# One order for the mixers' steps and the weight stream, set by an expected time per engine

## The reference

```
for l in range(2):                                   # second block
    p = rms_norm_2(h, norm_pre_mix[l]) @ w_in[l]     # 2048 x 7952
    o_ret  = retention_group(p_ret)
    o_hgrn = hgrn2_group(p_hgrn, ...)
    o_ml   = mlstm_group(p_ml, ...)
    o_rw, v_first = rwkv7_group(p_rw, v_first, ...)  # delta rule: a triangular solve in chunks of 128
    h = h + rms_norm_2(concat([o_ret, o_hgrn, o_ml, o_rw]) @ w_out[l], norm_post_mix[l])
    u = rms_norm_2(h, norm_pre_ffn[l])
    h = h + rms_norm_2((silu(u @ w_gate[l]) * (u @ w_up[l])) @ w_down[l], norm_post_ffn[l])
```

## Time and profile before

| | |
|---|---|
| device time, 3 runs | median 4277.95 us (4275.65 to 4281.48) |
| the profiled execution's own time | 4288.42 us |
| its span, first to last instruction | 4287.1 us |
| mean granted TensorE clock | 0.951 of full speed |
| HBM read | 623.04 MB, 146 GB/s over the span |

### The profile page before, as it was taken

The page is one execution under the profiler, slowest core; times in us unless marked ns, Lnnn a source line. Parts: engine busy times, 40 slices in busy tenths (PEclk is TensorE's granted clock), DMA queues, the critical chain, the costliest instruction groups (busy, mean ns, idle before and its releaser), DMA issues.

```text
span 4287.1 us, 57523 instructions
## 1 busy us (share of the span) xinstructions
PE 3928.6 (92%) x24004; PEld 3484.0 (81%) x24004; DVE 2291.8 (53%) x3630; ACT 1784.1 (42%) x2539; POOL 106.7 (2%) x61
## 2 busy tenths in 40 slices
PE   6999988998899899778999999989898779999998
PEld 5777766877688888558999988878787569999987
DVE  4455655566555554556555544565644665454444
ACT  4444534444443443324444444444433334444443
POOL 0000000000010000000000000010000000000000
PEclk9999999999999999869999999999999689999999
DMA  5555444554354433314666666544333136666665
GB/s 183 172 153 164 127 128 122 145 162 138 114 158 128 135 112 106 99 59 143 182 183 184 183 200 194 170 123 144 105 108 94 53 108 182 183 182 186 193 194 168
DMA packets 342084, 628.88 MB, mean 147 GB/s; under 512 B 21712, under 2 KB 64672, under 8 KB 340800
## 3 DMA queue, kind: packets, MB, share of 16 engines
q1 hardware_dynamic: 330888, 609.46, 47.8%
q10 hardware_dynamic: 10936, 15.75, 1.2%
HBM read 623.04 MB, written 2.10 MB: 146 GB/s over the span
## 4 chain that ended last, share of the span: by engine, by line
PE 78%; DVE 11%; ACT 6%; issue 2%; POOL 2%; ACTq 1%; DMA 0%; DVEq 0%; POOLq 0%
PE bank L453 66%; DVE weights_low L377 3%; ACT weights_high L375 2%; DVE arena L914 1%; PE bank L1076 1%; PE bank L1171 1%; PE bank L2191 1%; PE bank L2178 1%; PE bank L575 1%; PE bank L2190 1%; POOL stat L536 1%; DVE arena L1819 1%; PE bank L1079 1%; POOL arena L1786 1%; PE bank L1155 1%
## 5 line engine op out<-in xcount | busy, mean ns | idle before, releaser
L377 DVE TENSOR_TENSOR weights_low<-weights,weights_high 128x1024 fp32r<-128x1024 f32 (+4 forms) x1176 | 1399.2, 1193 | 1432.0 <-ACT weights_high L375 1425.3
L375 ACT ACTIVATE weights_high<-weights 128x1024 fp32r<-128x1024 f32 (+4 forms) x1176 | 1207.6, 1029 | 1275.7 <-PE bank L453 1246.6
L453 PE MATMUL bank<-x_high,weights_high 128*128 128x256 f32 x3776 | 1082.7, 287 | 28.2 <-DVE weights_low L377 12.3
L453 PE MATMUL bank<-x_low,weights_high 128*128 128x256 f32 x3776 | 1076.3, 285 | 0.0
L453 PE MATMUL bank<-x_high,weights_low 128*128 128x256 f32 x3776 | 1075.8, 285 | 0.0
L453 PEld LDWEIGHTS bank<-x_high,weights_high 128*128 128x128 f32 x3776 | 732.7, 194 | 38.1 <-DVE weights_low L377 25.0
L453 PEld LDWEIGHTS bank<-x_low,weights_high 128*128 128x128 f32 x3776 | 732.9, 194 | 0.0
L453 PEld LDWEIGHTS bank<-x_high,weights_low 128*128 128x128 f32 x3776 | 732.7, 194 | 0.0
L453 PE MATMUL bank<-weights_high,x_high 128*128 128x512 f32 (+3 forms) x1408 | 572.1, 406 | 69.2 <-DVE x_low L580 34.1
L453 PE MATMUL bank<-weights_high,x_low 128*128 128x512 f32 (+3 forms) x1408 | 547.1, 389 | 0.0
L453 PE MATMUL bank<-weights_low,x_high 128*128 128x512 f32 (+3 forms) x1408 | 546.7, 388 | 0.0
(11 more groups left out here) (377 smaller groups left out, 3677.4 us busy)
## 6 DMA issues: line engine op xcount, KB each, us to landing
weights<-in_w_in_dram SPq DMA_DIRECT2D x208, 512.0 KB, 3.7
weights<-in_w_ffn_gate_dram SPq DMA_DIRECT2D x176, 512.0 KB, 4.3
weights<-in_w_ffn_up_dram SPq DMA_DIRECT2D x176, 512.0 KB, 4.2
weights<-in_w_ffn_down_dram SPq DMA_DIRECT2D x176, 512.0 KB, 4.8
weights<-in_w_out_dram SPq DMA_DIRECT2D x128, 512.0 KB, 3.8
weights<-in_even_w_in_dram SPq DMA_DIRECT2D x88, 512.0 KB, 3.6
weights<-in_odd_w_in_dram SPq DMA_DIRECT2D x80, 512.0 KB, 3.7
weights<-in_mem_w_kv_dram SPq DMA_DIRECT2D x32, 512.0 KB, 4.4
```

Of the source, the lines that this page charges most:

```text
L375: dve.wait_ge(self.high_split.count(nc.scalar.activation(high, raw, ACT.Copy)))
L377: nc.vector.tensor_tensor(low, raw, high.bitcast(F32), ALU.subtract))
L453: ins = nc.tensor.matmul(out, l, r, start=(u == 0 and c == 0 and x + y == 0), stop=(u == blk.n - 1 and c == UNIT - 1 and y == 1))
```

## The change

**Expected time.** Each engine's queue (`Line`) gets a clock. Emitting an instruction adds a cost by its kind and its columns; counting up a semaphore records the clock plus 0.1 us as the expected time of that mark; a wait moves the waiting queue's clock up to it. `Matmuls` does this for PE.

**Pieces.** `step` now emits one bank of a unit instead of all of it: 6 matmuls of 512 or of 256 columns. The split of unit g+2 goes with a unit's first bank, the load of unit g+4 with its last; each bank of a block's last unit is evacuated as it is done.

**Order.** A task says before each of PE's waits which marks it will wait for (`yield wanted`); `rest` is gone, and a bare `yield` stands in its place. `weave` lets the stream go first only where `stream_first` says so: the task's marks are expected more than 0.7 us after the next piece could begin, or DVE's clock is over 3 us or ACT's over 2 us ahead of it. A bare `yield` so takes no piece of the stream unless DVE or ACT is ahead. `need` yields a constant that forces a piece each time. `fill` puts off a transpose whose mixer is expected to end more than 0.7 us after PE's clock, unless nothing else can go on. No computation changes, and no matmul, copy or transfer is added or removed.

```diff
+SLACK = 0.7
+DVE_LEAD, ACT_LEAD = 3.0, 2.0
+HOP = 0.1
+def expected_at(marks):
+    return max([expected.get((id(sem), value), 0.0) for sem, value in marks], default=0.0)
 class Line(Counter):
-    def __init__(self, eng, sem):
+    def __init__(self, eng, sem, start=0.16, column=0.00104):
     def wait_ge(self, *marks):
+        self.clock = max(self.clock, expected_at(marks))
+    def ran(self, ins):
+        n = columns(one.ins[0] if isinstance(one, mybir.InstTensorReduce) else one.outs[0])
+        self.clock += self.start + self.column * n * (6 if isinstance(one, mybir.InstReciprocal) else 1)
+class Matmuls(Line):
+    def matmul(self, out, lhsT, rhs, **flags):
+        self.clock += (n + 32) / 2400 if rhs.dtype == F32R else max(4 * n, 480) / 2400
+            self.act = Line(nc.scalar, sem("act_done"), 0.2, 0.00085)
+            self.pool = Line(nc.gpsimd, sem("pool_done"), 0.3, 0.0026)
-    def rest(self, us):
-        self.debt += us
-        while self.debt >= 1.3:
-            self.debt -= 1.3
-            yield
     def weave(self, task):
-        for _ in task:
-            self.fill()
-            stuck = 0 if self.step() else stuck + 1
+        for wanted in task:
+            if wanted == self.STREAM:
+                self.fill(True)
+                stuck = 0 if self.step() else stuck + 1
+                continue
+            self.fill(False)
+            while self.stream_first(wanted or []):
+                self.step()
+                self.fill(False)
+    def stream_first(self, wanted):
+        if self.g == len(self.units) or not self.can_run(*self.units[self.g]):
+            return False
+        marks = [self.load_mark[self.g] if blk.kind == "plain" else self.low_mark[self.g]]
+        begin = max(self.pe.clock, expected_at(marks))
+        return (expected_at(wanted) > begin + SLACK or self.dve.clock > begin + DVE_LEAD or self.act.clock > begin + ACT_LEAD)
     def fill(self, must):
-            if piece is not None and piece[0] in self.ended and self.blocks[piece[1]].done:
+            if piece is not None and piece[0] in self.ended and self.complete(piece[1]):
+                if not (must and i == 0) and expected_at(self.ended[piece[0]]) > self.pe.clock + SLACK:
+                    return
     def step(self):
-        self.g += 1
-        self.split(g + AHEAD)
-        marks = self.plain_unit(g, blk, u) if blk.kind == "plain" else self.matmul_unit(g, blk, u)
-        self.load(g + AHEAD + 2)
+        if n == 0:
+            self.split(g + AHEAD)
+        mark = self.plain_unit(g, blk, u) if blk.kind == "plain" else self.bank_matmuls(g, blk, u, n)
+        self.n += 1
+        if self.n == len(blk.banks):
+            self.g, self.n = g + 1, 0
+            self.load(g + AHEAD + 2)
         if u == blk.n - 1:
-            blk.done = [blk.evac(n, b, mark) for n, (b, mark) in enumerate(zip(blk.banks, marks))]
+            blk.done.append(blk.evac(n, blk.banks[n], mark))
...
+            yield [*self.bank_free[b]]
             pe.wait_ge(*self.bank_free[b])
-        yield from self.rest(3.0)
+        yield
...
-            if not (0 <= w < n and units[w].get("quiet")):
-                yield
```

More of the change, by code:

```diff
@@ L205 @@
     need: str = None
+    scale: object = None
     done: list = field(default_factory=list)
 class Program:
+    STREAM = "a piece of the stream"
     def __init__(self, nc, A, consts, out):
@@ L438, in matmul_unit, with bank_matmuls @@
+        return self.used_mark[g]
+    def bank_matmuls(self, g, blk, u, n):
+        pe, w, b = self.pe, blk.width, blk.banks[n]
         high, low = self.w_high[g % SPLIT], self.w_low[g % SPLIT]
[L439 to L456, removed]
@@ L1386, in indexer @@
             dve.wait_ge(dve.now())
-            yield from self.rest(1.4)
+            yield
         for t in range(T):
@@ L1634, in head_rms_gate @@
                 marks[t] = dve.did(nc.vector.tensor_tensor(tmp[:, t, :], tmp[:, t, :], gain, ALU.mult))
-            yield from self.rest(1.2)
+            yield
         for t in range(T):
@@ L1822, in hgrn @@
         exponents(0)
-        multiply(-1, k, q)
+        yield from multiply(-1, k, q)
         yield
@@ L1931, in mlstm @@
         yield
+        yield [m]
         pe.wait_ge(m)
@@ L2015, in rwkv @@
                 dve.seq(nc.vector.tensor_tensor(vc, vc, vf, ALU.add))
-                yield from self.rest(1.0)
+                yield
         else:
@@ L2080, in rwkv @@
             self.bank_free[b] = [m]
-        yield from self.rest(2.2)
+        yield
         L4 = L_.rearrange("p (n s) -> p n s", s=P)
@@ L2154, in rwkv @@
                     self.bank_free[b] = [m]
-                    yield from self.rest(0.9)
+                    yield
             for grp in range(2):
@@ L2270, in rwkv @@
         dve.seq(nc.vector.tensor_tensor(y3, y3, wide_st, ALU.subtract))
-        yield from self.rest(2.4)
+        yield
         act.wait_ge(dve.now())
@@ L2277, in rwkv @@
         dve.seq(nc.vector.tensor_tensor(y3, y3, wide_st, ALU.mult))
-        yield from self.rest(3.6)
+        yield
         dve.wait_ge(landed)
```

391 lines of the change are left out of this document (251 added, 140 removed).

## The result

| | before | after |
|---|---|---|
| median, 4 runs each | 4279.57 us (4275.65 to 4281.48) | 4109.95 us (4098.08 to 4116.59) |
| profiled execution | 4288.42 us | 4116.59 us |
| span | 4287.1 us | 4115.3 us |
| mean TensorE clock | 0.951 | 0.969 |

The ratio is 0.9602, 95% interval 0.9578 to 0.9625: 4.0 in 100 faster, 169.6 us by the medians, 171.8 by the profiled executions. The forecast was 4120.

What follows compares the result with a forecast made beforehand. PE was taken as the bound, busy 3928.6 of 4287.1 us. 151 + 32 + 43 - 70 = 156 us off the profiled 4288.4 gave 4132, or 4122 at the median, stated as 4120; range 4000 to 4262.

Steps and rivals of the forecast that it cites:

- part 3: hgrn and the first half of rwkv: finer pieces shorten what a mixer step waits behind; 32 of 94.6 us won.
- part 1: RWKV solves: stream only where PE would wait, so it fills the drains behind; 151 of 201.7 us won.
- rival 1: RWKV solve: the clock falls once the stream is thinned out there, slower than before, 4297 us; chance 0.10.
- rival 2: DVE becomes the bound: PE's waits for the stream's splits grow to some 75 us, +100, 4220; chance 0.16.
- rival 3: Everything is filled: drains give 180, the other two parts half of 238, slack costs 40; 259 off, 4020; chance 0.16.
- Part 2: Transposes behind mixers, mostly in the drains: putting them off removes 69 us of waits, already counted in the 151.
- part 4: The two attention layers with the memory: 43 us won of 143 idle and clock loss.
- Part 5: Some 850 places where PE can wait: SLACK leaves waits up to 0.7 us open, costing 70 us.
- rival 4: Mixers run ahead, then wait in `need` for inputs; the drains come back as long, no change; chance 0.04.

Runs made afterwards that it cites:

- The shift by itself: The kernel before, with only the two yields of each level of the RWKV solve taken out: 4217.6 us, ratio 0.9853.
- slack 0: The changed kernel with SLACK 0 for 0.7, so a piece goes in wherever PE would wait at all by the clocks: 4111.0 us, 0.9598.
- states fed: The changed kernel with one stream piece forced after each of the three steps of the chunk states behind the solve's levels: 4071.4 us, 0.9512.
- scaled thresholds: The changed kernel with expected costs of DVE, ACT and POOL halved, and SLACK and both leads halved too (0.35, 1.5, 1.0): 4332.9 us, 1.0120.

## Why the prediction was right, point by point

- **Sum.** Forecast 156 us off the profiled execution, measured 171.8; 4120 against 4110.0. By stages it had 43 for the attention layers, less their part of the 70 for slack, and the rest for the two blocks; measured were 45.2 and 135.1 (126.6 with the FFNs' ends). The terms in the third layer's block, by the table above: hgrn up to the solve lost 16.7 us less (16 forecast, half of part 3), and behind the solve 66.1 less (75.5 forecast, half of part 1).
- **Luck in it.** The 70 us for slack were not what was lost. What stands in their place is about 36 us of clock behind the solve's levels, which no term of the sum had (rival 1 came near it), and 21 us of short waits. The sum is near the mark because one term was too dear by about what another had left out.
- **Part 1, the shift.** Right in place and mechanism. I had the levels at 5.2 us with no stream between them; the trace has the whole 18 us stretch as one run, 5.7 us a level (48 records of 0.118). The amount was too small: 57.6 us a block, the levels' stream alone, where the stretch became 79 us shorter; the earlier trace rows already had 118 of its 200 us as stream. The shift by itself is 64.5 us in the old kernel, not 151. The rest of what the drains gave back came only with the new order; what that order needs is the next point.
- **What I missed.** The leads. I weighed DVE_LEAD only as a risk (rival 2), and named the waits as what brings the gain. Without the leads the time is 4324. My working of two units' time, 5.42, less 2.22 for a split, against a lead of 3.0, should have led to the question what the order is without it. The forecast came out right since the lead was in the change. That the costs must be right within some tens of 100 also stood only as a remark under rival 3.
- **Part 2, late transposes.** The forecast put nothing on top for them, yet said that `fill` makes PE do other steps instead. The experiment shows that they carry nothing that can be told: 4115.6. Of the waits of 69 us, 33.0 go with the shift alone and 36.0 with the order by expected time.
- **Part 3 and part 4.** 32 and 43. Not separable from the leads by these runs; the stretch up to hgrn, 45.2, agrees with part 4, and the 16.7 us above with part 3. The clock at the ends of NSA and of differential attention is lower than it was: 540 to 700 is at 0.86, where 540 to 720 was at 0.91.
- **Part 5, the slack.** Too dear. Waits of kinds that last 1.1 us at most add up to 37.8 us in 66 before and 58.7 in 91 after: 21 us, not 70, and a slack of 0 wins nothing back. The step that failed is the count: of 850 places only some 90 wait at all.
- **Rival 1, the slower one.** It came in part, in another place. The level loop, on which I put 125 us, kept its clock, as I had argued from its lack of waits. The states behind it lost it, about 36 us for both blocks by (1 - clock) x length x busy share (0.14 x 160 x 0.95 + 0.11 x 140 x 0.95), and 39 were won back by feeding them. The rule of the Trainium skill ("TensorE: Matmul & The Clock Gate", "A second HAM failure mode: psum-queue depth-cycling") blames pauses between groups; with slack 0 the clock fell and stayed low with no pause that the profile shows, so the trace with slack 0 doesn't bear that reason out. In the kernel after there were pauses of 0.38 and 0.47 us ahead of the fall, so they may have a part there; a fall without them is shown.
- **Rival 2.** Waits for the split rose by 16.7 us, a sixth of its price. Rivals 3 and 4 didn't come; rival 3's reason, that the costs fit, holds.
- **Signs.** These came: levels at 5.7 us, stream matmuls in mlstm's attention, no waits left for the gates, and idle time that didn't move to the layers' ends. The FFNs are 4 us longer each. These did not:
  - No 20 us window at half clock without transfers was to be left, and 1490 to 1510 is one, as is 640 to 660 (clock 0.50, DMA share 0.00).
  - Waits for the split were not to be over 45 us; they are 61.9.
  - PE's waits were to be more in number. They are 150 for 170, 1.5 us on average for 2.0; only the short ones are more.
  - A fall of PE's busy time by less than 60 us was to mean that the clock's part was not won. It fell by 46.5. By that sign the forecast fails in its clock half: 125.3 of the 171.8 us are idle time, and the states took back some of the clock that the drains gave. With the states fed busy time is 3849.3, 79.3 below the kernel before.

Still open: what in the states' matmuls lets the clock go, since no run changed one thing about them alone; which of DVE's and ACT's lead carries the 214 us, and what they would bring without the rule for waits; why scaled thresholds win back 163 of 386 and not more. The 39 us of the fed states are divided in the main: between the two profiled executions PE's busy time fell by 32.8 us and its idle time by 11.6 (the mean clock, 0.969 to 0.977, is 33 us of 4115).

## What to carry to other kernels

Where one engine sets the time and filler work is at hand, look where the filler is spent: in a loop that is double-buffered and keeps the engine busy by itself it is wasted, and it is missing later. An order by expected times needs two conditions, not one: filler where the engine would wait, and filler when another engine has run ahead, since the filler's own preparation queues there; and its costs have to be near: 1.3 times the right ones lost 71 us here, half of them 386. After such a change look at the clock again: work that the filler had covered can lose it.

## What the runs showed of the hardware

TensorE's clock went from 2.4 to 1.2 GHz while the profile shows the engine never idle. With slack 0 PE is busy for 20.00 us of the 20 from 1480 to 1500; in the first ten the clock is at 1.00, and in the second, in a run of 48 float32 matmul records of 64 columns, it falls (0.57 over the ten). From 1490 to 1515 it is at 0.59 with 25.00 of 25 busy. Dense matmuls of 128 x 128 held it at 1.00 for 18 us with nothing else. More pieces of the stream between the narrow matmuls went with a higher clock: (1 - clock) x length over the four places is 36 us in the kernel after, 26 with slack 0, 11 with one piece after each step and 7 with two.
